# Attention bias tables loaded from GpSimd's queue, in a loop of its own, instead of SyncE's

## The reference

```
x += 0.5 * SwiGLU_1(rms(x))
x += Mixer_l(rms(x))      # l = 0: gated linear attention || chunk-band attention; l = 1: forgetting attention
x += 0.5 * SwiGLU_2(rms(x))

def band_attention_sample(q, k, v, ck, cv, rel_bias):     # 8 heads, 512 cached rows
    kk = jnp.concatenate([ck, k], axis=1)
    s = jnp.einsum('bihd,bjhd->bhij', q, kk) * (D ** -0.5)
    p = jax.nn.softmax(s + bias[None], axis=-1)
    return jnp.einsum('bhij,bjhd->bihd', p, vv)

def fox_sample(q, k, v, logf, ck, cv, clogf):             # 16 heads, 1024 cached rows
    fk = jnp.concatenate([-c_after, fq], axis=1)
    s = jnp.einsum('bihd,bjhd->bhij', q, kk) * (D ** -0.5)
    s = s + fq.transpose(0, 2, 1)[..., :, None] - fk.transpose(0, 2, 1)[..., None, :]
    p = jax.nn.softmax(jnp.where(valid, s, -jnp.inf), axis=-1)
    return jnp.einsum('bhij,bjhd->bihd', p, vv)
```

## Time and profile before

| | us |
|---|---|
| median of 3 runs | 2955.0 |
| the three runs | 2955.0, 2948.9, 2955.4 |
| span of the profiled execution | 2944.9 |
| band stage | 778 to 904 |
| fox stage | 2088 to 2400 |

### The profile page before, as it was taken

The page is one execution under the profiler, slowest core; times in us unless marked ns, Lnnn a source line. Parts: engine busy times, 40 slices in busy tenths (PEclk is TensorE's granted clock), DMA queues, the critical chain, the costliest instruction groups (busy, mean ns, idle before and its releaser), DMA issues.

```text
span 2944.9 us, 48416 instructions
## 1 busy us (share of the span) xinstructions
PE 2773.1 (94%) x19827; PEld 2646.2 (90%) x19827; DVE 739.6 (25%) x1751; ACT 708.7 (24%) x973; POOL 944.0 (32%) x285
## 2 busy tenths in 40 slices
PE   7999999999779999999999999999777789999997
PEld 7999999998548999999999999999545579999997
DVE  4110114323543211112211012311234433110112
ACT  2221222210242222122222122211244432221221
POOL 3443444330003344344344344432000013443442
PEclk9999999996699999999999999999899999999998
DMA  3212212112242221221221221222677832212211
GB/s 130 71 68 89 72 59 85 64 51 95 100 175 75 72 82 65 82 71 63 92 75 67 78 73 61 93 87 91 236 269 279 286 135 72 71 68 85 76 53 69
DMA packets 52873, 293.49 MB, mean 100 GB/s; under 512 B 8065, under 2 KB 11922, under 8 KB 28722
## 3 DMA queue, kind: packets, MB, share of 16 engines
q1 hardware_dynamic: 52786, 292.24, 28.1%
HBM read 279.95 MB, written 12.27 MB: 99 GB/s over the span
## 4 chain that ended last, share of the span: by engine, by line
PE 85%; DMA 5%; issue 4%; DVE 3%; ACT 1%; POOL 0%; SPq 0%; DVEq 0%; ACTq 0%
PE ps L306 75%; DMA s_bias<-neg_f_dram 4%; PE ps L670 4%; PE ps L932 1%; PE ps L984 0%; PE ps L922 0%; PE ps L1274 0%; DMA p_bias<-neg_f_dram 0%; DVE xn_lo L407 0%; PE ps L1263 0%; PE ps L372 0%; PE ps L1249 0%; PE ps L1269 0%; PE ps L912 0%; POOL w_lo L292 0%
## 5 line engine op out<-in xcount | busy, mean ns | idle before, releaser
L292 POOL TENSOR_TENSOR w_lo<-w_raw,w_hi 128x2048 fp32r<-128x2048 f32 (+2 forms) x185 | 791.7, 4279 | 1132.5 <-ACT w_hi L287 1124.2
L306 PE MATMUL ps<-xn_hi,w_hi 128*128 128x320 f32 x3616 | 829.8, 311 | 19.1 <-POOL w_lo L1641 10.9
L306 PE MATMUL ps<-xn_lo,w_hi 128*128 128x320 f32 x3616 | 827.4, 310 | 0.0
L306 PE MATMUL ps<-xn_hi,w_lo 128*128 128x320 f32 x3616 | 826.3, 310 | 0.0
L306 PEld LDWEIGHTS ps<-xn_hi,w_hi 128*128 128x128 f32 x3616 | 606.9, 189 | 21.6 <-POOL w_lo L1641 10.9
L306 PEld LDWEIGHTS ps<-xn_lo,w_hi 128*128 128x128 f32 x3616 | 607.8, 189 | 0.0
L306 PEld LDWEIGHTS ps<-xn_hi,w_lo 128*128 128x128 f32 x3616 | 607.6, 189 | 0.0
L287 ACT ACTIVATE w_hi<-w_raw 128x2048 fp32r<-128x2048 f32 (+2 forms) x185 | 326.6, 1766 | 533.5 <-PE ps L306 444.1
L559 POOL TENSOR_TENSOR h_lo<-prod,h_hi 128x640 f32 x88 | 139.1, 1581 | 716.5 <-ACT h_hi L512 716.5
L306 PE MATMUL ps<-h_hi,w_hi 128*128 128x320 f32 x1408 | 320.9, 309 | 0.0
L306 PE MATMUL ps<-h_hi,w_lo 128*128 128x320 f32 x1408 | 320.8, 309 | 0.0
(11 more groups left out here) (187 smaller groups left out, 2073.9 us busy)
## 6 DMA issues: line engine op xcount, KB each, us to landing
w_raw<-in_w_up SPq DMA_DIRECT2D x87, 1024.0 KB, 4.7
k_cache<-in_fox_kc SPq DMA_DIRECT2D x16, 2048.0 KB, 13.6
v_cache<-in_fox_vc SPq DMA_DIRECT2D x32, 1024.0 KB, 9.2
w_raw<-in_w_down_a SPq DMA_DIRECT2D x32, 768.0 KB, 4.3
w_raw<-in_w_in SPq DMA_DIRECT2D x24, 1024.0 KB, 4.7
w_raw<-in_w_down_b SPq DMA_DIRECT2D x32, 640.0 KB, 3.8
k_cache<-in_band_kc SPq DMA_DIRECT2D x8, 1024.0 KB, 7.0
v_cache<-in_band_vc SPq DMA_DIRECT2D x8, 1024.0 KB, 5.8
```

The source lines that it names most:

```text
L292: nc.gpsimd.tensor_tensor(out=w_lo[:, slot, 0:cols], in0=w_raw[:, slot, 0:cols], in1=w_hi[:, slot, 0:cols].bitcast(F32), op=ALU.subtract). ...
L306: last = nc.tensor.matmul(ps[:, 2 * unit + half, 0:HALF], w_part[:, slot, w:w + P], a_part[:, k, half * HALF:(half + 1) * HALF], start=k = ...
```

## The change

SyncE's list no longer loads s_bias and p_bias. A new method `Attention.pool` issues the same transfers, with the same sources, targets and semaphores, from GpSimd's queue: the first three in front of a loop, then in a loop over the passes s_bias for u = 1, s_bias for u = 0 of the next pass, and the two p_bias of the next pass, each behind a wait for the maximum that frees its buffer. These waits are one step earlier than SyncE's were: behind the maximum (L1073, L1113), not behind the small negation that follows it. In the even phase GpSimd enters it when the gated linear attention's output is split (gla_olo), in the odd phase right behind its memset of qz. ACT_ORDER is only wrapped at another place.

```diff
@@ Attention.sp @@
-                def bias(u):
-                    if not first or u:
-                        sp.wait_ge(self.smax_step, i * 4 + 2 * u)
-                    loads["bias"](i, u)
-
-                def prompt_bias():
-                    for hh in range(2):
-                        wait(self.max_step, i * 16 + (2 * hh - 2))
-                        sp.dma_start(p_bias[:, hh, :], self.prompt_bias(i, hh)).then_inc(self.bias_loaded[hh], 16)
-
                 keys(0)
                 if first:
                     if space_free:
                         keys(1)
                         value_chunk(0, 0)
                         space_free()
-                    bias(0)
-                    prompt_bias()
...
                 else:
                     keys(1)
-                    bias(0)
                     value_chunk(0, 0)
-                    prompt_bias()
                     if self.chunks == 2:
                         value_chunk(0, 1)
-                bias(1)
                 for ch in range(self.chunks):
                     value_chunk(1, ch)
...
+        def pool(self, pool, load_bias):
+            def prompt_bias(i, hh):
+                pool.dma_start(p_bias[:, hh, :], self.prompt_bias(i, hh)).then_inc(self.bias_loaded[hh], 16)
+
+            load_bias(0, 0)
+            prompt_bias(0, 0)
+            prompt_bias(0, 1)
+            with pool.Fori(0, self.loops - 1) as i:
+                pool.wait_ge(self.smax_step, i * 4 + 1)
+                load_bias(i, 1)
+                pool.wait_ge(self.smax_step, i * 4 + 3)
+                load_bias(i + 1, 0)
+                for hh in range(2):
+                    pool.wait_ge(self.max_step, i * 16 + (13 + 2 * hh))
+                    prompt_bias(i + 1, hh)
+            pool.wait_ge(self.smax_step, 4 * self.loops - 3)
+            load_bias(self.loops - 1, 1)
...
+    def fox_bias(pool):
+        def load(i, u):
+            pool.dma_start(s_bias[:, 0:PAST], after_dram[bass.ds(i * H_C + 8 * u, 8), :].unsqueeze(1)
+                           .broadcast_to([8, DEC_SEQ, PAST])).then_inc(fox.sbias_loaded[u], 16)
+            pool.dma_start(s_bias[:, PAST:PAST + P], neg_f_dram[8 * u:8 * u + 8, SEQ:T].unsqueeze(1)
+                           .broadcast_to([8, DEC_SEQ, P])).then_inc(fox.sbias_loaded[u], 16)
+        return load
...
                 if ph["kind"] == "even":
                     gla_pool(pool, ph)
+                    pool.wait_ge(g_olo, H_A)
+                    band.pool(pool, band_bias(pool))
                 else:
                     pool.wait_ge(f_scratch, 32)
                     pool.wait_ge(logf_stored, 16)
                     fox.clear_queries()
+                    fox.pool(pool, fox_bias(pool))
```

More of the change, by code:

```diff
@@ L789, in trunk_program @@
                  ).split()
-    ACT_ORDER = ("C0 E2 sC0a sC0b sC0c C1 E3 C2 H0 E4 sE1 C3 E5 sH0 C4 H1 E6 sC1a sC1b sC1c C5 E7 Q+ C6 W H2 sE0+ "
-                 "C7 E0+ E1+ sH1 H3").split()
+    ACT_ORDER = ("C0 E2 sC0a sC0b sC0c C1 E3 C2 H0 E4 sE1 C3 E5 sH0 C4 H1 E6 sC1a sC1b sC1c C5 E7 Q+ C6 W H2 "
+                 "sE0+ C7 E0+ E1+ sH1 H3").split()
     class Attention:
@@ L1160, in values, with band_bias @@
                          ).then_inc(band.sv_loaded[slot], 16)
[L1162 to L1166, removed]
+        return dict(keys=keys, values=values)
+    def band_bias(pool):
+        def load(i, u):
+            pool.dma_start(s_bias[:, 0:WIN + P], ins["band_bias_s"][bass.ds(i * 2 + u, 1)]
+                           .rearrange("o p c -> p (o c)")).then_inc(band.sbias_loaded[u], 16)
+        return load
     def fox_loads(sp):
```

## The result

| | us |
|---|---|
| after, median of 4 runs | 2971.2 (2970.5 to 2973.0) |
| before, median of 4 runs | 2953.6 (2948.9 to 2955.4) |
| ratio after / before | 1.0064, 95% interval 1.0047 to 1.0081 |
| span of the profiled execution, after | 2969.8 (before 2944.9) |

The forecast was 2933 us, 0.75% less. The time lies above the whole range, on the other side.

A forecast was written before the change was run, and what follows sets the result against it. It took fox's passes to be bound by waits for s_bias, issued behind the keys on SyncE's one queue. From 2955.0 us, -17.6 (waits and start), -5.4 (clock) and +0.7 (GpSimd issue) gave 2933 us, range 2923 to 2948.

The forecast's parts named there:

- (1): Fox loop: s_bias on its own queue lands some 6 us after issue, removing its waits; 16.1 us gained.
- where s_bias was early: Fox pass 6: s_marks began 0.1 us after the last logits, taken as the lag without a wait for s_bias.
- (3): Fox, sM0 to sM1: without the long waits TensorE's clock stays full; 5.4 us gained, bounds 0 and 5.4.
- (2): Start of fox: biases issued before the keys bring the first s_marks 2.4 us earlier; 0.9 us lost at the second keys.
- the clock stays low: Rival for fox: the waits go but the clock gains nothing, (3) being 0; 2938 us, chance 0.11.
- (4): Band's start: GpSimd's issues, taken as 1 us each, delay three transfers in a row; 0.7 us lost, bounds 0 and 2.3.
- (5): SyncE, rid of 64 bias issues and their waits, gains nothing by itself; keys lose at most 1.7 us to s_bias.
- The room of 2.5 us: Fox loop: keys expected at 2243.5, wanted by the logit matmuls at 2246.0, so their delay was to cost nothing.
- A second queue gains nothing but issue time: Rival: DMA engines work in issue order whatever the queue, s_bias lands as late as now; 2953 us, chance 0.12.
- Slower: Rival: GpSimd takes long for each transfer, turning the change slower at about 5.8 us each; 2968 us, chance 0.07.
- s_bias still releases s_marks: Sign in the profile after, in fox, that the rival of a second queue gaining nothing holds.

The follow-up runs named there:

- e3: The changed kernel with fox's key loads cut into four transfers each, rows of 4 KB instead of 16 KB; 2938.3 us.
- e9: The changed kernel with s_bias's source rows stored twice, so it uses 16 DMA engines instead of 8; 2926.3 us, 0.9903 of before.
- e7: The kernel before with only fox's s_bias moved to GpSimd's queue, p_bias and band's biases staying on SyncE; 2972.3 us.
- e2: The kernel before with only fox's p_bias moved to GpSimd's queue, s_bias and band's biases staying on SyncE; 2959.3 us.
- e8: The changed kernel with band's biases back on SyncE and s_bias's source rows stored twice (16 engines); 2917.7 us, 0.9880 of before.
- e6: The kernel before with SyncE issuing s_bias between the two key loads of a pass, not behind them; 2934.5 us.
- e10: The kernel before, all on SyncE, with s_bias over 16 engines and issued between the two key loads; 2922.7 us, 0.9892 of before.
- e5: The kernel before with fox's s_bias in the loop issued from ScalarE's queue, behind the exponential; 2983.5 us.

## Why the prediction was wrong, point by point

**(1) The wait for s_bias: wrong, and it decided the sign.** The step that failed reads: "576 KB take about twice their own 1.7 us while keys are in flight, plus issue and completion: landed some 6 us after issue". It took 15.0 us for the 512 KB and 19.6 us to the end. Without keys in flight the 6 us were about right (6.6). Three things were wrong beside keys. It shared the engines by bytes, half and half; they share by packets, and 4 KB against 16 KB gave the queue 12% of the engines' time (e3 undid this: 13.9 us). It had s_bias on 16 engines; an 8-row source uses 8, which doubles the turns that each has to wait (e9 undid this: 13.95 us). And issue and completion were given some 2.6 us, where 3.4 us passed before the first packet moved. That p_bias follows s_bias in GpSimd's queue mattered little: without it (e7) the flights of passes 2 to 7 are 18.8 to 19.8 us, with it 19.3 to 19.6. Each of the two remedies alone was enough, since the logits ended 15.3 us after the issue (2173.79 + 0.1 against 2158.55): only what a flight has beyond some 15 us costs anything. Instead of -16.1 us the term is +17.5.

What I should have seen in the profile of before: the order of issue protects a short transfer as well as it delays it: in one queue s_bias stood behind the keys, but once they were through it had no keys beside it. The prediction priced only the delay.

It also misread pass 6 as one "where s_bias was early". From sM1 of pass 5 to sM0 of pass 6 the granted clock was 0.91, where those before passes 2, 3, 4, 5 and 7 had 1.00, and the stretch was some 1.7 us longer than those are without their waits. s_bias's 512 KB landed at 2321.2, no sooner after the issue than in other passes; the logits were late there (2321.31) and hid it. So the clock had cost something in one place that term (3) doesn't count.

**(2) Start of fox: right, and better than said.** From the first key issue to the first s_marks 3.7 us were gained, not 2.4, and the 0.9 us taken off again for the second keys were not lost: 11.42 us from sM0 to sM1 of pass 0. p_bias no longer stood in the way, as told. p_bias alone isn't enough: in e2, which leaves s_bias on SyncE, that wait is gone as well, but from the first key issue (2084.38) to the first s_marks (2098.75) it is 14.4 us, a gain of 1.3, and s_marks is 1.7 us behind the logits. The rest of the gain came with s_bias's early issue.

**(3) The clock: the link was right, the sign followed (1).** Stretches of 17.7 to 18.7 us where passes waited 4.5 to 5.1 us; 16.06 to 16.08 us in passes 2 to 6 of e8 and e9, where nothing waits. The seven stretches are 128.1 us after, 119.3 before and 112.1 without waits: it was +8.8 instead of -5.4, and the full term would have been -7.2. The rival "the clock stays low" is out. In e6 they stayed at 120.8 us with hardly a wait for s_bias in passes 1 to 7; I put that down to its 18.5 us of waits for p_bias, since with these down to 1.0 us in e10 they take 112.1.

**(4) Issue on GpSimd: too dear, and the wrong thing priced.** 0.55 to 0.73 us each, not 1. But band's start cost 3.0 us of wait and not 0.7, because p_bias was in use 5.1 us after the first of its two issues was through (some 780.5) where I carried over the 2.8 us of SyncE's queue. The waits placed one step earlier gained nothing: GpSimd's issue began 2.0 us after s_marks (2156.55), SyncE's 1.7 us after it in pass 1 of before.

**(5) What SyncE is rid of: nothing, as told, for the queue's time.** k_cache went from a median of 13.6 to 15.9 us to landing, 2.3 us more, against the 1.7 us allowed for; it is not waited for after pass 0. The room of 2.5 us held.

**The rivals.** "A second queue gains nothing but issue time" (2953 us) was nearest in kind, and too kind: it let s_bias land as late as now. The sign given for it (s_bias still releases s_marks) came true without it, since a later s_bias shows the same sign. "Slower" (2968 us) was nearest in number, by luck: it had GpSimd slow per transfer, from 5.8 us on; the issues measured a tenth of that, so that case was right in sign and wrong in cause. (Its sum at 4 us a transfer is -13.3 us, not -14.) A rival was missing: the two queues share by turns, and the small packets lose. The prediction quotes the rule of turns, packet by packet, and reads it as help for s_bias, "a short transfer overtakes a backlog", without asking how long the turns of the other queue are. An estimate after the fact: in 2163 to 2170 a key packet took 0.86 us (89.5% of 16 engines for 7 us, over 116 packets). 128 rows on 8 engines are 16 turns, 14 us, and with the 3.4 us until the first packet moves that makes some 17, where 15.0 was measured. It leaves out the rows' own time and that the keys ran out before the end, so it gives the size and no more.

## What to carry to other kernels

Moving a load to another queue doesn't move it out of the traffic. Before doing it, count the turns: packets of the transfer per engine, times the length of the other queue's packets. A short transfer with small packets beside long ones with large packets can as well be placed right in one queue, ahead of what it must not wait for (e10 was as fast as e9), and everything behind the new place must be looked at too (e6). And look at the slowest dimension of the source: 8 rows meant half of the engines, and storing them twice was worth 17 us with one queue (single runs) and 45 to 49 with two (2971.2 against 2926.3 and 2922.1). The fastest kernel, e8, has both: fox's biases on the second queue and the rows stored twice.

## What the runs showed of the hardware that I had not expected

- Two queues under load get like numbers of packets with data on the engines that both use, whatever their sizes: 119 of 4 KB against 106 of 16 KB with all engines in use. With an 8-row source it is 62 against half of 116 (GpSimd's queue) and 50 against half of 134 (ScalarE's), if half is what went through the same engines.
- In 7 us with two queues active, keys and biases together moved 308 (after), 318 (e9) and 343 GB/s (e5), where keys alone moved 437.
- With a source of 8 rows half of the packets of GpSimd's queue were under 512 B (in after 89 of 267 in 2163 to 2170, 16 of 241 with 16 rows); with ScalarE's queue it was 16 of 200. On which engines they were isn't shown.
- Beside keys, the first packet of the second queue moved only 3.4 us (GpSimd) and 4.1 us (ScalarE) or more after the issue began.
- A key load split in four costs SyncE 0.6 us for each issue (4.72 us for eight), and that alone made a kernel 20 us slower where something is queued behind it.
- ScalarE's queue was no better than GpSimd's: 20.2 to 20.8 us a flight.
